# S5 recurrence: the states turned back are not summed on GpSimd, TensorE takes four products, ScalarE writes a negated sine copy

## The reference

```
h_t = a * h_(t-1) + B u_t          (a, h complex; 32 groups of 64 states)
y_t = Re-part: h_re C_re - h_im C_im + d u_t
y   = gelu(y);  the last h_re, h_im are outputs too
```

## Time and profile before

| | before |
|---|---|
| three runs | 1576.66, 1579.38, 1590.64 us; median 1579.38 |
| the profiled execution | 1574.58 us |
| its span | 1572.9 us |
| mean granted TensorE clock | 0.916 |
| busy: PE, DVE, ACT, POOL | 1322.5, 963.1, 560.0, 633.5 us |

### The profile page before, as it was taken

How to read it: one execution, slowest core, us unless ns; L and a number is a source line. 1 busy time by engine, 2 the same in 40 slices (tenths; PEclk the granted TensorE clock), 3 DMA queues, 4 the chain that set the end, 5 groups by cost and what they waited for, 6 DMA issues and landing times. The chain is left out here.

```text
span 1572.9 us, 26564 instructions
## 1 busy us (share of the span) xinstructions
PE 1322.5 (84%) x7035; PEld 1043.9 (66%) x7036; DVE 963.1 (61%) x2027; ACT 560.0 (36%) x1019; POOL 633.5 (40%) x515
## 2 busy tenths in 40 slices
PE   3555999999976647999999762999999999999485
PEld 2444788888853425888888641787888887888231
DVE  7957655566539945455556454685554685675198
ACT  1115222332231224222222112685544685675132
POOL 2721332222207841344444333475434275465340
PEclk7777999999988977999999875999999999999797
DMA  9896112111245246444445742899776699895696
GB/s 235 284 320 201 54 57 72 58 53 53 101 124 74 83 132 241 165 174 182 165 160 179 210 139 87 301 370 376 271 267 240 217 376 387 296 382 195 259 415 254
DMA packets 178988, 322.83 MB, mean 205 GB/s; under 512 B 21925, under 2 KB 107221, under 8 KB 178670
## 3 DMA queue, kind: packets, MB, share of 16 engines
q1 hardware_dynamic: 154658, 271.59, 50.7%
q0 software_dynamic: 13664, 45.70, 7.8%
q10 hardware_dynamic: 10612, 4.87, 1.4%
HBM read 235.73 MB, written 86.39 MB: 205 GB/s over the span
## 5 line engine op out<-in xcount | busy, mean ns | idle before, releaser
L2160 POOL TENSOR_TENSOR down_lo<-expert_raw,down_hi (+1 forms) x64 | 155.4, 2449 | 182.4 <-ACT down_hi L2250 182.4
L2296 DVE TENSOR_TENSOR up_lo<-expert_raw,up_hi (+1 forms) x128 | 166.0, 1356 | 20.2 <-ACT up_hi L2245 20.0
L697 PE MATMUL ps_up<-up_hi,xT_hi 128*128 x400 | 161.6, 404 | 2.9 <-DVE up_lo L2296 2.9
L699 PE MATMUL ps_up<-up_hi,xT_lo 128*128 x400 | 157.5, 394 | 0.0
L698 PE MATMUL ps_up<-up_lo,xT_hi 128*128 x400 | 157.0, 393 | 0.0
L2245 ACT ACTIVATE up_hi<-expert_raw (+1 forms) x128 | 125.8, 1063 | 3.4 <-DMA expert_raw<-in_w 1.8
L697 PE MATMUL ps_out<-wout_hi,catT_hi 128*128 128x512 f32 (+1 forms) x272 | 110.8, 407 | 1.7 <-DVE catT_lo L1740 1.6
L698 PE MATMUL ps_out<-wout_lo,catT_hi 128*128 128x512 f32 (+1 forms) x272 | 108.9, 400 | 0.0
L699 PE MATMUL ps_out<-wout_hi,catT_lo 128*128 128x512 f32 (+1 forms) x272 | 108.7, 400 | 0.0
L852 POOL TENSOR_TENSOR v<-v,lng 128x512 f32<-128x512 f32 (+1 forms) x17 | 21.9, 1288 | 195.2 <-DVE v L1001 195.2
L2290 DVE TENSOR_TENSOR xT_lo<-ps_xT,xT_hi 128x512 fp32r<-128x512 f32 x102 | 65.7, 685 | 52.6 <-ACT xT_hi L2238 52.4
(11 more groups left out here) (394 smaller groups left out, 3267.2 us busy)
## 6 DMA issues: line engine op xcount, KB each, us to landing
expert_raw<-in_w SPq DMA_DIRECT2D x96, 1024.0 KB, 9.6
expert_rows<-yo SPq DMA_DIRECT2D x49, 512.0 KB, 8.2
wada<-in_w_ada SPq DMA_DIRECT2D x12, 2048.0 KB, 9.2
x<-in_x_prompt SPq DMA_DIRECT2D x32, 512.0 KB, 4.2
expert_rows<-blank SPq DMA_DIRECT2D x31, 512.0 KB, 4.1
x_rows<-x SPq DMA_DIRECT2D x16, 512.0 KB, 2.7
moe_in_rows<-h SPq DMA_DIRECT2D x16, 512.0 KB, 2.9
x<-x_rows SPq DMA_DIRECT2D x16, 512.0 KB, 11.9
```

The lines of the kernel that those rows point to most:

```text
L697: pe.matmul(out, left(0, k), right(0, k), start=k == 0, stop=False)
L699: last = pe.matmul(out, left(1, k), right(0, k), start=False, stop=k == n - 1)
L2160: pool.tensor_tensor(down_piece(down_lo, run, m), raw_piece(run, 2, m, 1), down_piece(down_hi, run, m).bitcast(F32), ALU.subtract).then_in ...
L2296: dve.tensor_tensor(up_piece(up_lo, run, m), raw_piece(run, m // 2, m % 2, KD // 2), up_piece(up_hi, run, m).bitcast(F32), ALU.subtract).t ...
```

## The change

GpSimd no longer sums. `h_re` and `h_im` keep the first product of each, and the second products stay in `back`, which now has two places. TensorE adds `back` as moving data to the same sum in `ps_b`, with the same tables `m_re` and `m_im`, from column NSEQ + 1 on. The sign of the real part comes from a negated copy of the sine, `neg`, which ScalarE writes, two pairs ahead: for pairs 0 and 1 at the start, for pair k+2 between the wait on `y_mm` of pair k and its GELUs. GpSimd still sums the one last column, for the final states, and its loop is written out. TensorE waits for the products (`ph`), not for the sums.

```diff
-        back = sb(st, "back", [P, 2, NCH])
+        back = sb(st, "back", [P, 2, 2, NCH])
+        neg = sb(st, "neg_turn", [P, 2, NCH])
...
                 def outputs(k):
                     if k == 0:
                         pe.wait_ge(toep_in, 16 * Q)
-                    pe.wait_ge(h_ok, 2 * (k + 1))
+                    pe.wait_ge(ph, 2 + 4 * (k + 1))
...
                     for h, m in ((h_re, S.m_re), (h_im, S.m_im)):
                         for g in range(2):
                             r = slice(g * ST, (g + 1) * ST)
-                            last = pe.matmul(pB[:, g, 0:CH], m[r, k, 1:9, :].rearrange("p k o -> p (k o)"), h[r, k, 0:CH],
-                                             start=False, stop=h is h_im)
+                            pe.matmul(pB[:, g, 0:CH], m[r, k, 1:9, :].rearrange("p k o -> p (k o)"), h[r, k, 0:CH],
+                                      start=False, stop=False)
+                    for i, m in enumerate((S.m_re, S.m_im)):
+                        for g in range(2):
+                            r = slice(g * ST, (g + 1) * ST)
+                            last = pe.matmul(pB[:, g, NSEQ + 1:CH], m[r, k, 1:9, :].rearrange("p k o -> p (k o)"),
+                                             back[r, k % 2, i, 0:NCH - 1], start=False, stop=i == 1)
...
                 pe.wait_ge(fin_ok, 2)
+                pe.wait_ge(h_ok, 2 * PAIRS)
...
+                def negate(k):
+                    act.wait_ge(turn_in[k % 4], 16 * (k // 4) + 16)
+                    act.activation(neg[:, k % 2, :], turn[:, k % 4, 1, :], ACT.Copy, scale=-1.0).then_inc(neg_ok, 1)
+
+                negate(0)
+                negate(1)
...
                 for k in range(PAIRS):
                     act.wait_ge(y_mm, k + 1)
+                    if k + 2 < PAIRS:
+                        negate(k + 2)
...
                     pool.wait_ge(scan_ok, 2 * k + 4)
-                    p.did(pool.tensor_tensor(re, scan[:, b, 0, :], C, ALU.mult))
-                    p.did(pool.tensor_tensor(im, scan[:, b, 0, :], N, ALU.mult))
-                    p.did(pool.tensor_tensor(back[:, 0, :], scan[:, b, 1, :], N, ALU.mult))
-                    p.link(pool.tensor_tensor(back[:, 1, :], scan[:, b, 1, :], C, ALU.mult))
+                    pool.wait_ge(neg_ok, k + 1)
+                    if k >= 2:
+                        pool.wait_ge(y_mm, k - 1)
+                    p.did(pool.tensor_tensor(h_re[:, k, NSEQ + 1:CH + 1], scan[:, b, 0, :], C, ALU.mult))
+                    p.did(pool.tensor_tensor(h_im[:, k, NSEQ + 1:CH + 1], scan[:, b, 0, :], N, ALU.mult))
+                    p.did(pool.tensor_tensor(back[:, b, 0, :], scan[:, b, 1, :], neg[:, b, :], ALU.mult))
+                    p.link(pool.tensor_tensor(back[:, b, 1, :], scan[:, b, 1, :], C, ALU.mult))
                     pool.sem_inc(h_free, 1)
-                    pool.tensor_tensor(re, re, back[:, 0, :], ALU.subtract).then_inc(h_ok, 1)
-                    pool.tensor_tensor(im, im, back[:, 1, :], ALU.add).then_inc(h_ok, 1)
+                    for i, h in enumerate((h_re, h_im)):
+                        pool.tensor_tensor(h[:, k, CH:CH + 1], h[:, k, CH:CH + 1], back[:, b, i, NCH - 1:NCH], ALU.add).then_inc(h_ok, 1)
```

More of the change, by code:

```diff
@@ L1065, in s5 @@
         y_mm, y_ok, t_mm, r_ok, y_out, f_mm, f_ok, f_out, fin_ok = sem("y_mm"), sem("y_gelu"), sem("y_turned"), sem("y_rows_ready"), sem("y_stored"), sem("final_mm"), sem("final_copied"), sem("final_stored"), sem("sample_state")
-        h_free = sem("scan_free")
+        h_free, neg_ok = sem("scan_free"), sem("neg_turn_ready")
         WIDTH = (P, P, NSEQ)
@@ L1316, in pair @@
                     C, N = turn[:, q, 0, :], turn[:, q, 1, :]
-                    re = h_re[:, ds(k, 1), NSEQ + 1:CH + 1].rearrange("p o c -> p (o c)")
-                    im = h_im[:, ds(k, 1), NSEQ + 1:CH + 1].rearrange("p o c -> p (o c)")
                     pool.wait_ge(scan_ok, 2 * k + 4)
-                    p.did(pool.tensor_tensor(re, scan[:, b, 0, :], C, ALU.mult))
-                    p.did(pool.tensor_tensor(im, scan[:, b, 0, :], N, ALU.mult))
-                    p.did(pool.tensor_tensor(back[:, 0, :], scan[:, b, 1, :], N, ALU.mult))
-                    p.link(pool.tensor_tensor(back[:, 1, :], scan[:, b, 1, :], C, ALU.mult))
+                    pool.wait_ge(neg_ok, k + 1)
[5 more added lines that the diff above has]
+                    p.link(pool.tensor_tensor(back[:, b, 1, :], scan[:, b, 1, :], C, ALU.mult))
                     pool.sem_inc(h_free, 1)
-                    pool.tensor_tensor(re, re, back[:, 0, :], ALU.subtract).then_inc(h_ok, 1)
-                    pool.tensor_tensor(im, im, back[:, 1, :], ALU.add).then_inc(h_ok, 1)
+                    for i, h in enumerate((h_re, h_im)):
+                        pool.tensor_tensor(h[:, k, CH:CH + 1], h[:, k, CH:CH + 1], back[:, b, i, NCH - 1:NCH], ALU.add).then_inc(h_ok, 1)
                     pool.wait_ge(h_ok, 2 * k + 2)
[L1329 to L1333, removed]
+                for k in range(PAIRS):
+                    pair(k, k % 2, k % 4)
 def mixout(nc, S, a):
```

## The result

The changed kernel is faster: median 1565.9 us (12 runs, 1561.3 to 1576.1) against 1578.5 us (12 runs, 1576.0 to 1591.9) before. The ratio is 0.9915, 95% interval [0.9894, 0.9936], a gain of 12.6 us. The prediction was 1573.3 us, range 1567 to 1583: the right direction and in the main the right mechanism, but 6.1 us where about twice as much came, and the median lies 1.1 us under the range.

What follows compares the result with a forecast made beforehand. VectorE's pace, slowed by GpSimd, bounds before; TensorE bounds after: 488.7 + 69.9 + 2.8 + 0.6 + 0.9 = 562.9 against 569.0, gain 6.1 us, so 1573.3 us, range 1567 to 1583.

Steps and rivals of the forecast that it cites:

- What bounded before: Recurrence of s5: VectorE's own work sets the pace, 5.61 us per pair, with 1.70 us of excess beside GpSimd's arithmetic.
- GpSimd's sums slow the scans: VectorE's two scans, 2.05 us beside GpSimd's sums, should return to 1.27 us, 0.78 us less per pair.
- TensorE becomes the bound: With the added matmuls TensorE's pair takes 4.75 us, slightly above VectorE's 4.7 us.
- the 0.6 us for ScalarE: ScalarE's negation and GELU delay the next Toeplitz product: 0.1 us allowed for each of six pairs without transposes.
- the prediction's own rival: TensorE is faster than summed, so VectorE's 4.7 us bounds: end at 558.7, gain 10.3, 1569 us; chance 0.08.
- Price of the added matmuls: TensorE's four matmuls on back per pair cost 1.05 us, scaled from the h matmuls; 16 pairs give 16.8 us.
- the one open wait: Between outputs(13) and (14) TensorE has neither additions nor transposes, so it waits 0.9 us for ScalarE.
- The run of TensorE: TensorE works from the Toeplitz tables' landing at 488.7 to the end of outputs(15) at 562.9; its operations sum to 69.9 us.
- the prediction's 4.83: VectorE's pace per pair with scans freed: 5.61 - 0.78 = 4.83 us, before a third of L1275's 0.49 us came off.
- the rival of contention that only moves: GpSimd's products fall beside scans and sums, VectorE stays at 5.61 us per pair: change +0.6, 1580 us; chance 0.15.
- Half clock: TensorE at 1.2 GHz from 488.7 to 494.3 loses 2.8 us, then full clock; rival (0.09): three later such pairs, 1587 us.
- The chance of being slower by over 1%: 0.05, needing four or more pairs of TensorE at half clock, or unpaired matmuls with more on top.

Runs made afterwards that it cites:

- sums of one column: Kernel before the change with GpSimd's two sums cut to the last column and nothing else: median 1565.4 us, ratio 0.9922 to the kernel before.
- sums and matmuls: Changed kernel with GpSimd's sums of all 256 columns put back, TensorE waiting for them, the four matmuls kept: 1576.3 us, ratio 0.9998 to before.
- halved tables: Changed kernel with the Toeplitz tables loaded in two halves, outputs(0) waiting for the first half only: 1565.2 us, ratio 0.9904 to before.
- extra matmuls: Changed kernel with four unused matmuls of 264 columns on TensorE in its idle time ahead of outputs(0): 1565.5 us (one run).

## Why the prediction was right or wrong

**What bounded before: right.** VectorE's pace, slowed by GpSimd. The kernel before with sums of one column gives the whole gain (12.9 us) with no other change, all but about 1 us of it by VectorE's faster pairs.

**GpSimd's sums slow the scans: right**: 1026 ns with them and 685 without, where nothing else was changed. The 1019 ns of the kernel with sums and matmuls arose beside other work of GpSimd and adds no proof. The Trainium skill (GPSIMD Engine Reference, Key points) names contention with VectorE instructions that have two SBUF inputs; these runs agree (sums and scans in SBUF were slowed, VectorE's products with one input in PSUM kept 0.41 to 0.42 us in every profile), and add that both sides pay: a scan beside a product went from 0.64 to about 0.88 us and the product from 0.73 to 1.22 us.

**TensorE becomes the bound: right, but with luck.** Twice the added matmuls cost 13.8 us, and the outputs ran with one gap of 0.9 us. Yet the margin that the prediction gave it, 4.75 against 4.7 us, was not there. With the measured 0.86 us TensorE's pair is 3.7 + 0.86 = 4.56 us, and its chain, without the 0.6 us for ScalarE, would end at 559.3; VectorE's chain at 4.7 us ends at 558.7 by the prediction's own rival, and at 4.8 us, its pace with halved tables or extra matmuls, at 559.9. TensorE bounds only because VectorE came out faster still, for a reason that the forecast did not have (below). Where that reason was absent VectorE bounded, and the run length was the same 94.2 to 94.5 us.

**Price of the added matmuls: mis-sized.** I read 0.55 + 0.54 us for the four `h` matmuls and scaled it. Each of the two held 0.1 us that belongs to its end of the row, next to Toeplitz or next to the additions, and that comes once per pair with or without more matmuls. Measured 0.86 us for 1.05, 3.0 us over 16 pairs. The Trainium skill (TensorE: Matmul & The Clock Gate, Part 3), by which an estimate from the same rows gave 1.08 us, was right that the row groups overlap: 2.16 us would have been the price without.

**ScalarE: right for the negation** (0.416 us for 0.44) **and for the one open wait** (0.89 us for 0.9), too high for the six pairs behind additions: 0.6 us allowed, no such wait. The wait in question:

```profile
553.95 0.60 PE L1177 MATMUL ps_b<-back,m_im 64*128 64x255 f32 x4
554.59 0.42 ACT L1228 ACTIVATE neg_turn<-turn 128x256 f32<-128x256 f32 x1 [2.99 <-PE ps_b L1177]
...
554.91 0.65 ACT L1244 ACTIVATE uT<-ps_b 128x264 f32<-128x264 f32 x2
...
555.43 1.13 PE L1168 MATMUL ps_b<-uT,toep 128*128 128x264 f32 x4 [0.89 <-ACT uT L1244]
```

**The run of TensorE.** Foretold 74.2 us from the landing of the tables (488.7 to 562.9), measured 70.9, so 3.3 less. The two terms above make 3.6; the 0.3 the other way lies in the many small terms and was not traced.

**The time before: the step that failed most.** The step that failed is "562.9, against 569.0 now. Gain 6.1 us": the sum was made against the end of outputs(15) in a single profile, and the gain was carried to the median. But the two kernels depend on different starts. Before, the run starts with VectorE's pair 0, that is when TensorE has turned the rows; the changed kernel's run starts when the tables land. The profile of before had an entry 3.1 us shorter than the second one (17.7 to 20.8), and so showed 3 us less to gain than usual, while its tables landed at the usual time. With the usual entry the whole stage takes 128.0 us before and 115.8 or 115.5 changed, 12.4 us less, against the 12.6 us of the medians. 6.1 + 3.1 + 3.0 + 0.6 = 12.8, less the 0.3 above, closes the sum. So of the 6.5 us that were missing, 3.1 are the time before, 3.0 the added matmuls and 0.6 ScalarE, less the 0.3.

**VectorE's pace: 4.7 us foretold, 4.5 in the changed kernel**, but by another way. The prediction's 5.61 was taken from pair 1 to pair 14. In that measure the pace is 4.80, 4.82 and 4.88 us in the three experiments where GpSimd follows the scans directly (4.73, 4.76 and 4.81 from pair 0 to 15), and 4.60 and 4.54 in the two profiles of the changed kernel. The 4.88 is the prediction's 4.83, without the third of L1275's 0.49 us that it gave back: L1275 kept its 911 ns. In the changed kernel GpSimd starts pair 2 late, because that pair's negation stands behind outputs(0) on ScalarE. From there on many of its products lie beside the scans:

```profile
498.00 0.73 POOL L1337 TENSOR_TENSOR h_re<-scan,turn 128x256 f32<-128x256 f32 x1 [5.88 <-ACT neg_turn L1228]
```

The wait was 5.9 and 5.3 us in the two profiles of the changed kernel and 4.1 without the added matmuls (paces 4.43 to 4.51 us), 2.2 with extra matmuls ahead and none with the halved tables (4.76 and 4.73 us). It shows in how far GpSimd's first product lies behind the end of the pair's scans from pair 3 on: 0.1 to 0.2 us with sums of one column, extra matmuls or halved tables, 2.6 to 5.1 in the changed kernel and without the added matmuls. So the phase goes with this wait. In the changed kernel GpSimd also waits for a negation in eight or nine later pairs, which keeps it late; without the added matmuls it stays late with no further wait. No run changed the wait alone, so that it is the cause is inferred. It is the rival of contention that only moves: it did move, and cost less in its new place than in the old.

**Half clock: right.** Outputs(0) at 1.2 GHz (491.44 to 497.23, 5.8 us), then full clock to the end of the stage. Its removal gives nothing, since VectorE bounds then; the 2.8 us in the sum were a term of TensorE's chain with another chain of the same length beside it.

**The chances.** 0.93 for within 1% holds (0.85%, interval 0.64 to 1.06%), though the point was at half of the gain. The chance of being slower by over 1% was tied to four pairs at half clock; by the prediction's own 4.75 us a pair four give 12.9 us and not 16, so it takes five.

## What to carry to other kernels

Take the start of each chain from more than one profile when a change moves the bound from one engine to another: the old chain and the new one may hang on different events, and chance in one of them goes fully into the difference. Price added matmuls by the middle members of a row of equal ones, not by the first or the last, which took 0.1 us more here; where the row has only two members, as here before the change, both carry it. Where VectorE and GpSimd work on SBUF together, count the overlaps by pairs of instructions: taking two sums off GpSimd made VectorE's pair 0.68 us shorter here, with VectorE's list unchanged. And when two chains end within a microsecond of each other, say that either may bound.

## What was not expected of the hardware

Two instructions that contend do not share the loss in fixed parts. Beside VectorE's sums two GpSimd products (0.73 us alone) took 0.73 and 0.91 us and stretched the sums from 0.42 to 0.87 and 0.91; beside the scans the products took 1.22 and 1.11 us, and the two scans took 1.77 us instead of 1.27. The same four products cost VectorE 1.0 us per pair in the first place (867 + 911 - 2 x 420 + 2 x 685 - 1270 ns) and 0.5 us plus what little the sums lost in the second. Which of these places the loop settled in went with how late GpSimd was in one pair at its start. Why a wait of 2.2 us there was caught up within two pairs (extra matmuls) and waits of 3.2 and 4.1 us were not (sums and matmuls, no matmuls on `back`) stays open; these kernels differ in more than the wait.
